# Blocked up projection with its activations passed through DRAM, in one layer of a hybrid decoder

## The reference, cut to what matters

```python
def rmsnorm(x, g):
    xf = x.astype(jnp.float32)
    y = xf * lax.rsqrt(jnp.mean(xf * xf, axis=-1, keepdims=True) + EPS)
    return (y * g.astype(jnp.float32)).astype(x.dtype)
...
    x = x + merged @ w_out
    xn2 = rmsnorm(x, norm_mlp)
    x = x + jnp.square(jax.nn.relu(xn2 @ w_up)) @ w_down
    return x, C, n, m, kc, vc
```

## Time and profile before

| | |
|---|---|
| median of 3 runs | 1661.66 us (1661.43 to 1661.97) |
| the profiled execution: span | 1660.2 us |
| median less that span (what lies around it) | 1.5 us |
| MLP, first up matmul to last down matmul | 921.5 to 1650.1 us |
| PE busy | 1638.1 us, 99% of the span |
| DVE, ACT, POOL busy | 57%, 38%, 21% |
| DMA, mean | 60 GB/s |

### The profile page before, as it was taken

One profiled execution on the slowest core, in us unless ns is written; L12 is line 12 of the kernel. 1 busy time (PEld: TensorE's weight loads), 2 busy tenths in 40 slices (PEclk: granted clock), 3 DMA queues, 4 the chain that ended last, 5 costly groups with the idle time before them and its releaser, 6 DMA issues.

```text
span 1660.2 us, 26819 instructions
## 1 busy us (share of the span) xinstructions
PE 1638.1 (99%) x10049; PEld 1495.6 (90%) x10049; DVE 949.5 (57%) x1753; ACT 633.9 (38%) x1407; POOL 350.8 (21%) x351
## 2 busy tenths in 40 slices
PE   9999999999999999999999999999999999999997
PEld 8999999899998899888988899999999999999996
DVE  5413323443145445763545877767777677766787
ACT  5523334332235433553403543333344443343332
POOL 3002001010001100111001233333333222223354
PEclk9999999999999999999999999999999999999999
DMA  7104354462311132211241101111111111110113
GB/s 220 53 28 136 64 71 100 51 89 28 69 30 26 36 80 49 52 26 26 64 147 38 52 26 50 51 51 51 51 43 33 51 51 51 51 41 35 51 64 114
DMA packets 138793, 99.46 MB, mean 60 GB/s; under 512 B 82376, under 2 KB 128464, under 8 KB 138712
## 3 DMA queue, kind: packets, MB, share of 16 engines
q1 hardware_dynamic: 138712, 98.34, 24.4%
HBM read 88.43 MB, written 11.60 MB: 60 GB/s over the span
## 4 chain that ended last, share of the span: by engine, by line
PE 96%; DVE 1%; DMA 1%; issue 1%; ACT 1%; POOL 0%; SPq 0%; DVEq 0%; POOLq 0%; ACTq 0%
PE bank L913 37%; PE bank L1285 23%; PE bank L1318 6%; PE bank L1319 6%; PE bank L1317 6%; PE bank L1265 5%; PE bank L858 3%; PE bank L1326 2%; PE bank L1099 2%; PE bank L1069 1%; PE bank L970 1%; PE bank L978 1%; PE bank L973 1%; PE bank L1016 1%; DMA xin<-in_x_prompt 1%
## 5 line engine op out<-in xcount | busy, mean ns | idle before, releaser
L1285 PE MATMUL bank<-xT_hi,w_hi 128*128 128x384 f32 (+1 forms) x768 | 250.7, 326 | 1.0 <-DVE xT_lo L1886 1.0
L1285 PE MATMUL bank<-xT_hi,w_lo 128*128 128x384 f32 (+1 forms) x768 | 250.6, 326 | 0.0
L1285 PE MATMUL bank<-xT_lo,w_hi 128*128 128x384 f32 (+1 forms) x768 | 250.5, 326 | 0.0
L913 PE MATMUL bank<-xT_hi,w_hi 128*128 128x384 f32 (+1 forms) x1008 | 194.1, 334 | 0.0
L913 PE MATMUL bank<-xT_hi,w_lo 128*128 128x384 f32 (+1 forms) x1008 | 186.2, 326 | 0.0
L913 PE MATMUL bank<-xT_lo,w_hi 128*128 128x384 f32 (+1 forms) x1008 | 186.1, 326 | 0.0
L913 PEld LDWEIGHTS bank<-xT_hi,w_hi 128*128 128x128 f32 x1008 | 166.5, 188 | 4.3 <-issue 2.9
L2589 POOL TENSOR_TENSOR e<-gain_b,e 128x512 f32<-128x512 f32 x60 | 78.2, 1304 | 434.9 <-ACT gain_b L1815 434.9
L913 PEld LDWEIGHTS bank<-xT_lo,w_hi 128*128 128x128 f32 x1008 | 168.7, 188 | 0.0
L913 PEld LDWEIGHTS bank<-xT_hi,w_lo 128*128 128x128 f32 x1008 | 168.7, 188 | 0.0
L2369 DVE TENSOR_TENSOR x<-bank,x 128x512 f32<-128x512 f32 x210 | 142.1, 691 | 31.5 <-PE bank L1319 30.9
(11 more groups left out here) (275 smaller groups left out, 3010.2 us busy)
## 6 DMA issues: line engine op xcount, KB each, us to landing
raw<-in_w_in SPq DMA_DIRECT2D x64, 256.0 KB, 4.5
raw<-in_w_up SPq DMA_DIRECT2D x16, 1024.0 KB, 5.3
raw<-in_w_down SPq DMA_DIRECT2D x16, 1024.0 KB, 5.0
raw<-in_w_in SPq DMA_DIRECT2D x9, 1024.0 KB, 5.4
xin<-in_x_prompt SPq DMA_DIRECT2D x8, 512.0 KB, 5.2
bc<-gate_rows SPq DMA_DIRECT2D x32, 128.0 KB, 6.9
Cin<-in_state_C SPq DMA_DIRECT2D x4, 1024.0 KB, 8.1
out<-Cin SPq DMA_DIRECT2D x16, 256.0 KB, 8.6
```

The costliest lines, as they stand in the source:

```text
L913: last = nc.tensor.matmul(out, lhsT, rhs, start=(step == 0), stop=(step == 3 * KT - 1))
L1285: last = nc.tensor.matmul(bank[unit_bank(g, u)][:, 0:cn], w[:, 0, k * WCOLS + tile * P:k * WCOLS + (tile + 1) * P], x[:, k, c0:c0 + cn], s ...
```

## The change

The MLP becomes two phases.

Up phase: for each of the 16 groups the up projection itself is made of seven block products. Tokens are halved (512 + 512), D is halved (4 + 4 blocks of 128 rows), the 256 columns are halved. The sums of the token blocks (S1 to S4) are built once, tile by tile, while w_out ends (`round_next`, `rest_next`, `next_sums`, `round_sums`, `rest_sums`); the sums of the weight blocks (T1 to T4) are built by POOL for each group. P1, P2, P5, P6, P3, P7, P4 are 12 matmuls of 512 columns each; P6 and P7 add onto P1's bank after ACT has copied it, P3 onto P5's; P4 starts afresh in N's bank and T in P2's. N (sampled tokens) is 16 matmuls of 256 columns, T two small ones that turn its result. The 4 hidden blocks of a group are squared by ACT, DVE builds the sums S1 to S4 that the down projection will need, and all seven operands, hi and lo, go to DRAM: 7 stores of 512 KB a group, and 128 KB for the sampled tokens. The residual x2 goes to DRAM too (9 x 512 KB).

Down phase: x2 comes back as `y` (9 x 512 KB); eight chunks of two groups read their seven operands (1 MB each) and 2 MB of w_down; a unit is 6 matmuls of 512 columns, so a chunk has 28 such units and 2 units N of 8. All of PSUM is read by DVE. The last chunk is blocked as well.

The units of w_out are reordered, so that the first tiles of the last block come earlier (`OUT_SEQ`). The weights' loads, splits and sums, the loops (now written out in full) and the place of all buffers follow from this. The core of the diff:

```diff
+OUT_SEQ = [(cq, i) for cq in range(2) for i in range(NT)] + [(2, i) for i in range(4)]
+for _i in range(NT - 4):
+    OUT_SEQ += [(3, _i), (2, _i + 4)]
+OUT_SEQ += [(3, i) for i in range(NT - 4, NT)]
...
+UP_SEQ = ("P1", "P2", "N", "P5", "P6", "P3", "P7", "P4", "T")
+UP_BANK = {"P1": 0, "P6": 0, "P7": 0, "P5": 1, "P3": 1, "P2": 2, "T": 2, "N": 3, "P4": 3}
...
+            load_dn(0)
+            load_op(0)
+            sp.wait_ge(up_mm, up_done(NG - 1, "P7"))
+            for i in range(NT):
+                sp.dma_start(y[:, i, :], x2_dram[i]).then_inc(x2_back, 16)
+            load_op(1)
+            load_op(2)
+            load_op(3)
+            load_dn(1)
+            store_rest(NG - 1)
+            load_smp(0)
+            load_smp(1)
+            for k in range(4, 7 * NCH):
+                load_op(k)
...
+                elif name == "P3":
+                    pe.wait_ge(up_act, act_read(g, "P5"))
+                elif name == "P7":
+                    pe.wait_ge(up_act, act_read(g, "P6"))
...
+            norm_transposes(2 * NT - 2, ybuf2)
+            pe.wait_ge(norm_lo, 2 * (NT + HB))
+            pe.wait_ge(up_wh, 1)
+            pe.wait_ge(free_v, OUT_UNITS - 3)
+            first_unit("P1", False)
+            pe.wait_ge(up_wh, 2)
+            pe.wait_ge(free_v, OUT_UNITS - 1)
+            first_unit("P2", False)
+            norm_transposes(2 * NT - 1, ybuf2)
+            first_unit("P1", True)
+            first_unit("P2", True)
...
+                if name == "N":
+                    pe.wait_ge(norm_lo, 4 * NT)
...
+                if i >= 1:
+                    norm_tile(NT + i - 1, x2[:, i - 1, :], ybuf2)
+                if i >= 2:
+                    rest_next(NT + i - 2)
+                if i - 3 >= HB:
+                    rest_sums(i - 3)
+            norm_tile(2 * NT - 1, x2[0:rows_of(NT - 1), NT - 1, :], ybuf2)
+            rest_next(2 * NT - 2)
+            up_rest(0, 0)
+            up_rest(0, 1)
+            rest_sums(NT - 3)
+            rest_sums(NT - 2)
+            up_rest(0, 2)
+            up_rest(0, 3)
+            rest_next(2 * NT - 1)
...
+            def hidden_tail(g):
+
+                for n in (S1, S3, S2, S4):
+                    hidden_sum(g, n)
+                hidden_rest(g, A22)
+                hidden_rest(g, A12)
...
+                if g:
+                    hidden_tail(g - 1)
+                add_copy(g, "P2", f11[:, :], p1[:, :], "P1")
+                if g:
+                    hidden_rests(g - 1)
+                hidden_rest(g, A11)
+                if not later:
+                    up_rest(g + 1, 0)
+                    up_rest(g + 1, 1)
+                if g:
+                    dve.wait_ge(ops_out, 16 * 6 * g)
+                add_copy(g, "P3", af[:, A12, 1, :], u2[:, :], "P6")
...
+            for i in range(NT):
+                rms(NT + i)
+                if i - 2 >= HB:
+                    next_sums(i - 2)
+            for name in SUMS[0:3]:
+                up_sum_of(0, name)
+            next_sums(NT - 2)
+            up_sum_of(0, "T4")
```

More of the change, by code:

```diff
@@ L130 @@
[L130 to L148, removed]
-    out = []
[L150 to L159, removed]
+LAST_ORDER = [NT - 1, 0, 1, 4, 5, 2, 3, 6, 7]
@@ new lines, in up_unit @@
+            def up_unit(g, name):
+                up_wait(g, name)
+                out = bank[up_bank(g, name)]
+                if name == "N":
+                    for k in range(KT):
+                        for lo in (False, True):
+                            last = nc.tensor.matmul(out[:, 0:WCOLS], hs[:, k, :],
+                                                    up_part(g, lo)[:, k * WCOLS:(k + 1) * WCOLS],
+                                                    start=(k == 0 and not lo), stop=(k == KT - 1 and lo))
+                elif name == "T":
+                    for tile in range(2):
+                        last = nc.tensor.matmul(out[:, tile * NS:(tile + 1) * NS], nat_s[:, tile * P:(tile + 1) * P], sel,
+                                                start=True, stop=True)
+                else:
+                    n, b = OPERAND[name]
+                    for step, (k, w, x) in enumerate((k, w, x) for k in range(4) for w, x in UP_PASSES):
+                        last = nc.tensor.matmul(out[:, :], up_b(g, b, w)[:, k, :], up_a(n, x)[:, k, :],
+                                                start=(step == 0 and name in STARTS), stop=(step == 11),
+                                                skip_group_check=name not in STARTS)
+                last.then_inc(up_mm, 1)
@@ new lines, in first_unit @@
+            def first_unit(name, rest):
+                out = bank[up_bank(0, name)]
+                n, b = OPERAND[name]
+                if not rest:
+                    for step in range(8):
+                        nc.tensor.matmul(out[:, :], up_b(0, b, False)[:, step // 2, :],
+                                         up_a(n, step % 2 == 1)[:, step // 2, :], start=(step == 0), stop=False)
+                    return
+                up_wait(0, name)
+                for k in range(4):
+                    last = nc.tensor.matmul(out[:, :], up_b(0, b, True)[:, k, :], up_a(n, False)[:, k, :],
+                                            start=False, stop=(k == 3))
+                last.then_inc(up_mm, 1)
@@ new lines, in squares, with round_hidden @@
+            def squares(g, m, v):
+                act.wait_ge(hid_c, 4 * g + m + 1)
+                nc.scalar.activation(v, v, ACT.Relu).then_inc(act_chain, 1)
+                chain[0] += 1
+                act.wait_ge(act_chain, chain[0])
+                nc.scalar.activation(v, v, ACT.Square).then_inc(hid_sq, 1)
+            def round_hidden(g, n, v):
+                if n in (A11, A12, A22):
+                    act.wait_ge(hid_sq, 4 * g + {A11: 1, A12: 2, A22: 3}[n])
+                else:
+                    act.wait_ge(hid_s, 4 * g + {S1: 1, S3: 2, S2: 3, S4: 4}[n])
+                nc.scalar.activation(aop[:, n, 0, :], v, ACT.Copy).then_inc(hid_hi, 1)
```

1229 lines of the change are left out of this document (698 added, 531 removed).

## The result

The changed kernel takes 1693.2 us (median of 4 executions, 1687.4 to 1694.5) against 1661.6 for the kernel before: a ratio of 1.018, 95% interval 1.0166 to 1.0199. It is 31.7 us slower; 8 were forecast.

What follows compares the result with a forecast made beforehand. PE, busy 99% of the span, was taken as the bound. 1616.4 us without PE waits + 25 + 6 + 18 + 3 = 1668.4 of span, with 1.5 for the median 1670; range 1658 to 1685, with both rivals 1642 to 1698.

Steps and rivals of the forecast that it cites:

- main case: Whole kernel: the seams cost more than the blocks save, 1670 us, slower than before; chance 0.50.
- Matmuls removed, 43.8 us: MLP: up groups of 21.4 us and down chunks of 42.6 gain 43.8 us if PE never waits.
- The rival that the blocks save nothing: Matmuls: 512-column reads run slower out of the new buffers, 10 us; too small to stand alone, no chance of its own.
- Front, 25 us: Seam from w_out to up: PE waits before group 0's N for DVE's long list, 25 us, ends 15 and 32.
- Shared port: POOL's SBUF operations and DVE's with two SBUF inputs never run together; four POOL adds take 7.41 us instead of 5.06.
- Up loop, 6 us: Up phase: a round of 21.8 us against PE's 21.4, 0.4 extra for each of 14 groups, 6 us.
- The store sets the loop (1693): Up loop: late-landing stores hold P3's addition, 23.5 us a group, 29 us instead of 6, 1693 us; chance 0.15.
- Seam, 18 us: Seam from up to down: PE waits for loads of y and operands, 18 us, ends 12 and 26.
- Clock, 3 us: After three gaps on the path PE comes out at a lower clock: 3 us, from 0 to 8.
- Down loop, 0: Down chunks: DMA and DVE keep up, DVE needing 27 us in 42.6, so no extra cost.
- The overlap rival (1647): Seams: POOL's sums fall into DVE's waits and DMA keeps its pace, so 15 and 14 us, 1647 us; chance 0.32.

Runs made afterwards that it cites:

- e6: The change with, ahead of the up projection, token sums' rounding and rests later, N's input earlier, group 1's weight sums after group 0's weight rests; 1682.3 us.
- e13: The change with POOL's weight sums behind A11's rest, P3's addition ahead of the weight rests, two of these behind A22's and P4's additions; 1678.3 us.
- e1: The change with 129 small identity products put into five PE gaps, in front and at the seam; 1691.2 us.
- e3: The change with ACT's rounding and DVE's rests of token sums one tile later ahead of the up projection; 1689.2 us.
- e4: The change with the first down chunk's weights issued between group 14's stores, operand 1 before y's tiles 4 to 8, operand 4 before the last stores; 1691.5 us.
- e14: The change with e6's and e13's orders, and between the phases the first chunk's weights, operands and second chunk's weights issued earlier; 1667.1 us.
- e5: The change with POOL forming the next group's four weight sums only after DVE's rest of the running group's A11; 1691.7 us.

## Why the prediction was right or wrong

- *Direction.* Right: the seams cost more than the blocks save. The forecast's main case was right in kind; its size was short by 23 us, and no one term holds them: the front 7.5, the loop 10.1 (half stalls, half pace), the seam 4.6 and the end 3.4, less the 3 of the clock.
- *Matmuls removed, 43.8 us.* Confirmed nearly. An undisturbed group takes 21.74 us (21.4 forecast) and a chunk 42.55 to 42.94 (42.6): 16 x 0.34 + 8 x 0.15 = 6.6 us less gain. I had taken 0.2277 us from units of 12; by the group's period they run at 0.231, the value I had for the short units. The rival that the blocks save nothing is out: 37 us are there.
- *Front, 25 us.* The failed step, the term most short by itself. 32.5 came, just over the upper end of 32. The mechanism (DVE's long list, POOL among it, N's input last) was right and stood in the prediction, with its sum: 14.9 us for DVE's list alone, 30 with POOL's sums in line. The 25 counted on a part of them running side by side, which no row showed. N started 37.2 us after w_out's end, 30.1 behind PE's own 7.1: all in line. The other 2.4 us lie behind N's start, most of them N at the low clock. e6 shows that the order, not the amount of work, held 11 us.
- *Shared port.* The rows that I used held: 685 against 1178 ns for the same operation. Right also in front (5.17 for 1.88).
- *Up loop, 6 us.* The second step that failed: 11 us of stalls in the profiled execution (the 5 of pace are counted with the matmuls). I had spread 0.4 us on each group; in fact twelve groups lose almost nothing and three lose 1.4 to 7.8, in other groups in other executions (the loop took 334 to 347 us in runs that leave it alone). Of the round of 21.8 against 21.4 I had the sum and not that it is a ring: once late, a group hands its lateness on, until PE has waited for it (DVE's first rest starts 5.3 us after T in a group at pace, 6.41 and 10.09 in two long ones, 5.39 and 5.30 in the groups behind them).
- *The store sets the loop (1693).* The number was near by luck: it wanted 23.5 us in every group, and twelve of them took 21.7 to 21.9. Its sign came true in part: it was to decide from a landing of about 4 us, and the three long groups follow such landings, with P3's addition waiting on the DMA. But the landing does it only where the collision has made the rests late; e13 with later landings has no stall.
- *Seam, 18 us.* 22.6, inside 12 to 26, by partly other waits: P1's weights 9.3 instead of being hidden, P5's operand 2.5 instead of 13, operand 4 3.5 instead of 8.4, the rest slow matmuls. I had the load of the weights as ready early; they overwrite what P2 of the last group reads and go out behind the stores. The 358 GB/s that I weighed did not bind: 399 to 410 for 50 us. The Trainium skill itself (HBM Reference, "Specifications (TRN2)") says that a core that streams alone goes well above that share; the trace agrees.
- *Clock, 3 us.* It dropped to 0.57 to 0.92 in the stretches of the seam, as foreseen, but filling the gaps gave about 2 us: most of the slow matmuls stood in the shadow of other waits. N of group 0 ran slow in e1 too, so what its clock costs there, some 1.7 us at most by its length, stays open.
- *Down loop, 0.* The chunks in their stride hold it. The end doesn't: PE waits 2.01 us before the last chunk's N, which stands first there, for VectorE's rest of w_down, and that N runs at the low clock, 5.5 us instead of 3.75. Less a tail that is 1.6 us shorter, and with the chunks' pace, that makes the 3.4 of the table's last stretch.
- *The overlap rival (1647)* needed N within 22 us of w_out's end. It came after 37, and in the best order after 25.

## What to carry to other kernels

A change that takes matmuls out of a full PE is paid by the engines that feed it: write their queues out in order at each seam and look where the input of the next PE instruction stands: another order of three queues gave 11 us here for no work. Keep GpSimd's additions away from VectorE's two-input operations when both lie on one ring, and check that the new place doesn't close another; a ring that waits for a store needs slack for a late landing. Where the DMA engines are full across a phase change, count the bytes needed before the next phase's second block, not only the order of issue.

## What was not expected of the hardware

- Two-input operations of VectorE and GpSimd in SBUF that run side by side take nearly the sum of their times: three of each, 5.17 us on DVE in e3's front, against 1.88 alone and some 3.9 for GpSimd's three. A GpSimd memset of the same 128x512 takes 0.526 us against 1.29 for a subtraction and disturbs nothing.
- A loop in which such collisions meet the landing of stores scatters: four executions of the change lie within 7 us, four of e4 (same loop) within 16, while e13's lie within 3.3 and seven of e14 within 2.3. A ring alone doesn't: e5, where it sets the pace, stays within 2.7.
- Identity products raise the granted clock of a waiting stretch (0.75 to 0.94) and may buy nothing; where they end 1.83 us before the work that counts, most of that work ran at the low clock all the same (0.58).
